# Gated recurrence of a hybrid decoder step: score masks on 32-token diagonal blocks, log k kept, three level buffers, levels by GpSimd

## What is computed

```python
L = jnp.cumsum(lc, axis=2)
inter = jnp.einsum('bhtk,bhkv->bhtv', qc * jnp.exp(L), S)
diff = jnp.where(causal, L[:, :, :, None, :] - L[:, :, None, :, :], -jnp.inf)
A = jnp.einsum('bhtk,bhsk,bhtsk->bhts', qc, kc, jnp.exp(diff))
intra = jnp.einsum('bhts,bhsv->bhtv', A, vc)
L_end = L[:, :, -1:, :]
S = jnp.exp(L_end[:, :, 0, :, None]) * S + jnp.einsum('bhsk,bhsv->bhkv', kc * jnp.exp(L_end - L), vc)
```

## Time and profile before

| | |
|---|---|
| Median of three runs | 2465.13 us (2464.92 to 2468.68) |
| The profiled execution: its time | 2473.21 us |
| Its span, first to last instruction | 2471.3 us |
| Mean granted TensorE clock | 0.961 |
| PE matmul busy | 2330.7 us (94%) |
| DVE busy | 1298.9 us (53%) |
| POOL busy | 1087.2 us (44%) |
| ACT busy | 487.6 us (20%) |
| Chain that ended last | PE 84%, DVE 7%, issue 4%, SP's queue 4%, ACT 1% |

### The profile page before, as it was taken

How to read it: one execution, slowest core, us unless ns; L and a number is a source line. 1 busy time by engine, 2 the same in 40 slices (tenths; PEclk the granted TensorE clock), 3 DMA queues, 4 the chain that set the end, 5 groups by cost and what they waited for, 6 DMA issues and landing times.

```text
span 2471.3 us, 33961 instructions
## 1 busy us (share of the span) xinstructions
PE 2330.7 (94%) x10472; PEld 1793.0 (73%) x10472; DVE 1298.9 (53%) x1975; ACT 487.6 (20%) x916; POOL 1087.2 (44%) x1274
## 2 busy tenths in 40 slices
PE   8998987999998999999899989879999989999997
PEld 6775776677776777777676757667777767777775
DVE  0634687533456666671216347874333666666622
ACT  1534211211113101100125332112111121010002
POOL 0000724556663666734300008254666637676342
PEclk9999986999999999999999999869999999999998
DMA  6222110222212222222032211103221222121220
GB/s 214 80 73 61 39 73 1 104 77 77 77 52 98 85 71 82 80 70 83 35 122 84 81 44 39 73 1 113 77 77 69 69 98 85 68 85 68 77 71 38
DMA packets 51600, 183.60 MB, mean 74 GB/s; under 512 B 7234, under 2 KB 27970, under 8 KB 37762
## 3 DMA queue, kind: packets, MB, share of 16 engines
q1 hardware_dynamic: 50882, 178.49, 21.2%
q10 hardware_dynamic: 576, 3.36, 0.3%
HBM read 172.64 MB, written 9.18 MB: 74 GB/s over the span
## 4 chain that ended last, share of the span: by engine, by line
PE 84%; DVE 7%; issue 4%; SPq 4%; ACT 1%; DMA 0%; POOL 0%; DVEq 0%; ACTq 0%; POOLq 0%
PE ps L1154 23%; PE ps L1082 18%; PE ps L1192 16%; PE ps L857 14%; PE ps L1398 3%; PE ps L1325 1%; PE ps L878 1%; SPq L694 1%; SPq L706 1%; PE ps L1075 1%; DVE r L2171 1%; PE ps L1067 1%; SPq L699 1%; DVE xT L1945 1%; DVE r L634 1%
## 5 line engine op out<-in xcount | busy, mean ns | idle before, releaser
L857 PE MATMUL ps<-xT,wring 128*128 128x288 f32 (+2 forms) x1152 | 282.2, 408 | 1.4 <-DVE o_mla L2112 1.4
L857 PEld LDWEIGHTS ps<-xT,wring 128*128 128x128 f32 x1152 | 219.9, 191 | 62.5 <-issue 1.7
L634 POOL TENSOR_TENSOR r<-lq 128x288 f32<-128x288 f32 (+1 forms) x40 | 28.6, 715 | 530.1 <-PE ps L1426 530.1
L1154 PE MATMUL ps<-lq,mreg 128*128 128x288 f32 x1008 | 251.3, 406 | 0.0
L1154 PEld LDWEIGHTS ps<-lq,mreg 128*128 128x128 f32 x1008 | 191.5, 190 | 52.9
L1507 ACT ACTIVATE r<-ps 128x288 f32<-128x288 f32 (+7 forms) x268 | 113.3, 428 | 562.8 <-PE ps L1082 255.4
L1154 PE MATMUL ps<-xT,wring 128*128 128x288 f32 x672 | 169.8, 406 | 0.0
L1154 PEld LDWEIGHTS ps<-xT,wring 128*128 128x128 f32 x672 | 127.7, 190 | 35.3
L1082 PE MATMUL ps<-r,kbuf 128*128 128x288 f32 x576 | 143.6, 406 | 0.0
L2585 POOL TENSOR_TENSOR kbuf<-o_mla 128x288 f32<-128x288 f32 x42 | 33.3, 792 | 225.6 <-DVE o_mla L2350 225.6
L1082 PEld LDWEIGHTS ps<-r,kbuf 128*128 128x128 f32 x576 | 109.4, 190 | 30.2
(11 more groups left out here) (377 smaller groups left out, 4747.9 us busy)
## 6 DMA issues: line engine op xcount, KB each, us to landing
wring<-w_stream SPq DMA_DIRECT2D x100, 1024.0 KB, 4.9
side<-w_stream SPq DMA_DIRECT2D x18, 704.0 KB, 4.3
r<-pages_in SPq DMA_DIRECT2D x80, 128.0 KB, 2.1
vbuf<-w_stream SPq DMA_DIRECT2D x12, 512.0 KB, 3.7
r<-w_stream SPq DMA_DIRECT2D x12, 512.0 KB, 3.6
wring<-w_stream SPq DMA_DIRECT2D x8, 704.0 KB, 4.2
r<-w_stream SPq DMA_DIRECT2D x6, 704.0 KB, 4.2
mreg<-pages_in SPq DMA_DIRECT2D x32, 128.0 KB, 2.1
```

The source lines that it names most:

```text
L634: eng.tensor_tensor(hi, lhi, mid, ALU.subtract)
L857: mm = pe.matmul(out[0:w.shape[-1], a * 512:a * 512 + hi - lo], w, x[:, lo:hi], start=(k == 0), stop=(k == len(pairs) - 1))
L1154: mm = pe.matmul(up_sum[name], ws[:, k * P:(k + 1) * P], xs[:, k, :], start=(k == 0), stop=(k == HK - 1))
```

## The change

It does seven things.

1. The lower six score blocks (the diagonal and levels 1 to 16) are computed only inside the four 32-token blocks on the diagonal: 24 matmuls of 32x32 for a chunk, each with a 32-column weight tile, in place of the 128x128 ones. The levels 32 and 64 are computed only where they have a pair, in four more matmuls, in a bank of their own. A chunk has 28 matmuls where it had nine.
2. DVE masks 192 columns (L2196 in the changed kernel), sums them into 32 PSUM columns (L2199), and spreads the sum over its own blocks with a 0/1 multiply (L2205).
3. ACT copies the off-diagonal blocks into the scores, three small copies, and PE waits for `hg_full`.
4. log k is kept in place of k (minus the cumulated log f), so that the lower half of a level needs no multiply after its exponential; the k of the diagonal is exponentiated into `k_now`, the decay to the chunk's end by four activations with a bias.
5. There are three level buffers, so head 2's levels are formed during head 0.
6. POOL forms all levels of all heads; DVE has none, and the `late` order is gone. ACT's exponentials for heads 2 and 3 go behind the copies of steps 0, 1, 2, 7 and 10 to 13.
7. The masks in the constants shrink from 1024 to 320 columns, and `value_blocks` is one 64x1024 operation.

The core of the diff:

```diff
+SUB = 32
+N_DIAG = LEVELS.index(SUB) + 1
+LEV_BUF = (2, 0, 1, 2)
+LEVEL_STEPS = {0: (2, 0, 2), 1: (2, 2, 5), 2: (2, 5, 7), 10: (3, 0, 2), 11: (3, 2, 5), 12: (3, 5, 7)}
+END_STEPS = {7: 2, 13: 3}
...
                 lo, hi, _ = parts(out, half)
-                llo, lhi, mid = parts(logf[:, h, 0:n], half)
...
                 eng.tensor_tensor(hi, lhi, mid, ALU.subtract)
-                ins = eng.tensor_tensor(lo, mid, llo, ALU.subtract)
+                ins = eng.tensor_tensor(lo, alo, mid, ALU.add)
...
-                pe.matmul(out[0:w, 0:w], k_hg[:, h, t0:t1], q_hg[:, h, t0:t1], start=True, stop=True)
...
+                for v in range(N_DIAG if c < N_CHUNK else 1 + SMALL_LEVELS):
+                    for i in range(w // SUB):
+                        lo, hi = SUB * i, SUB * (i + 1)
...
+                        mm = pe.matmul(diag[lo:hi, v * SUB:(v + 1) * SUB], k, q, start=True, stop=True)
                 if c < N_CHUNK:
+                    m = lev[N_DIAG]
+                    for i in range(2):
+                        pe.matmul(off[SUB * i:SUB * (i + 1), 0:64], m[:, at + SUB * i:at + SUB * (i + 1)],
+                                  m[:, at + 64:at + P], start=True, stop=True)
...
+                    if c < N_CHUNK:
+                        act.wait_ge(*hg_scores.at(l, n + 1))
+                        full, off = scores_hg[:, n % 2, :], bank[2 * (n % 2) + 1]
+                        copy(full[0:64, 64:P], off[0:64, 0:64])
+                        for a in (0, 64):
+                            ins = copy(full[a:a + SUB, a + SUB:a + 64], off[a:a + SUB, 64:64 + SUB])
+                        ins.then_inc(hg_full.sem, 1)
+                    if n in LEVEL_STEPS:
+                        decays_levels(*LEVEL_STEPS[n])
+                    if n in END_STEPS:
+                        decays_ends(END_STEPS[n])
...
+                    summed = bank[2 * (n % 2)][0:w, N_DIAG * SUB:(N_DIAG + 1) * SUB]
+                    dve.tensor_reduce(summed, masked[0:w, 0:nl, :].rearrange("p l t -> p t l"), AX_X, ALU.add
+                                      ).then_inc(hg_summed.sem, 1)
...
                 for n in range(N_HG + 1):
-                    h, c = divmod(n, N_CHUNK + 1)
-                    late = n < N_HG and c == 0 and h >= 2
...
+                    if n < N_HG:
+                        pair_sums(n)
+                    if n >= 1:
                         update(n - 1)
...
+                pool.wait_ge(*pool_d_ready.at(l, POOL_GROUPS))
+                differences(l, 2)
+                scaled(l, 2)
+
+                pool.wait_ge(*hg_upd.at(l, N_CHUNK + 2))
+                ends(l, 2)
+                value_blocks(l, 1)
+                ends_scaled(l, 2)
+                differences(l, 3)
+
+                pool.wait_ge(*hg_upd.at(l, 2 * (N_CHUNK + 2)))
+                ends(l, 3)
+                value_blocks(l, 2)
+                scaled(l, 3)
+                ends_scaled(l, 3)
```

More of the change, by code:

```diff
@@ L617, in parts, with levels @@
             return v[:, :, 0:half], v[:, :, half:2 * half], v[:, :, half - 1:half]
-        def levels(h, first=0, end=len(LEVELS)):
+        def levels(h, first, end):
+            b = LEV_BUF[h]
             for v in range(first, end):
-                half = LEVELS[v]
+                yield LEVELS[v], level[b][v], 0, SEQ
                 if v < SMALL_LEVELS:
-                    yield half, level_small[h % 2][:, v, :], T
-                else:
-                    yield half, level_big[h % 2][:, v - SMALL_LEVELS, :], SEQ
@@ L628, in level_differences @@
-        def level_differences(eng, h, first, end):
-            for half, out, n in levels(h, first, end):
+                    yield LEVELS[v], level_s[b][v], SEQ, T
+        def level_differences(eng, h, first=0, end=len(LEVELS)):
+            for half, out, t0, t1 in levels(h, first, end):
                 lo, hi, _ = parts(out, half)
-                llo, lhi, mid = parts(logf[:, h, 0:n], half)
-                mid = mid.broadcast_to([P, n // (2 * half), half])
+                _, lhi, mid = parts(logf[:, h, t0:t1], half)
+                alo, _, _ = parts(log_k[:, h, t0:t1], half)
+                mid = mid.broadcast_to([P, (t1 - t0) // (2 * half), half])
@@ L648, in ends_scaled, with level_scaled @@
-        def ends_scaled(eng, h):
-            eng.tensor_tensor(decayed[:, h % 2, 0, :], decayed[:, h % 2, 0, :], q_hg[:, h, :], ALU.mult)
-            return eng.tensor_tensor(decayed[:, h % 2, 1, :], decayed[:, h % 2, 1, :], k_hg[:, h, :], ALU.mult)
+        def level_scaled(eng, h, first=0, end=len(LEVELS)):
+            for half, out, t0, t1 in levels(h, first, end):
+                _, hi, _ = parts(out, half)
+                _, qhi, _ = parts(q_hg[:, h, t0:t1], half)
+                ins = eng.tensor_tensor(hi, hi, qhi, ALU.mult)
+            return ins
@@ L1022, in hg_pair_scores @@
-                if c < N_CHUNK:
-                    for v in range(SMALL_LEVELS, top - 1):
-                        m = big[:, v - SMALL_LEVELS, t0:t1]
-                        pe.matmul(out[:, (v + 1) * P:(v + 2) * P], m, m, start=True, stop=True)
-                    o = top * P
-                    m = big[:, top - SMALL_LEVELS, t0:t1]
-                    pe.matmul(out[:, o:o + P], m, m, start=True, stop=True)
-                    half = LEVELS[top]
+                diag, off = bank[2 * (n % 2)], bank[2 * (n % 2) + 1]
@@ L2481, in value_blocks @@
[L2481 to L2488 removed]
+                level_differences(pool, h).then_inc(lev_diff.sem, 1)
@@ L2836, in shape_constants @@
     s, t = np.arange(P)[:, None], np.arange(P)[None, :]
-    c[:, C_MASK:C_MASK + P] = s == t
-    for v, half in enumerate(LEVELS):
-        same = s // (2 * half) == t // (2 * half)
-        at = C_MASK + min(v + 1, len(LEVELS) - 1) * P
-        c[:, at:at + P] += same & (s % (2 * half) < half) & (t % (2 * half) >= half)
+    inside = SUB * (s // SUB) + np.arange(SUB)[None, :]
+    c[:, C_MASK:C_MASK + SUB] = s == inside
+    for v in range(N_DIAG - 1):
+        half = LEVELS[v]
+        at = C_MASK + (v + 1) * SUB
+        c[:, at:at + SUB] = ((s // (2 * half) == inside // (2 * half)) & (s % (2 * half) < half)
+                             & (inside % (2 * half) >= half))
+    c[:, C_BLOCKS:C_BLOCKS + P] = s // SUB == t // SUB
     tok = np.arange(T)
```

241 lines of the change are left out of this document (116 added, 125 removed).

## The result

The changed kernel takes **2391.64 us** (median of four runs, 2390.33 to 2393.01). Four runs of the kernel before have a median of 2466.49, which makes 74.9 us less. The later runs bear it out: there the kernel before had medians of 2470.1 to 2472.4, and the changed kernel, run again, a ratio of 0.9679. I had said 43 less. The direction was right and the size was not: the recurrence saves 41 us a layer, where I had worked out 21.5.

What follows compares the result with a forecast made beforehand. PE's queue and its waits bound the kernel, with DVE the fuller engine in the recurrence: PE's queue 27.5 us shorter a layer, less 6 of POOL waits, nets 21.5, 43 in all; 2465.1 becomes 2422 us, range 2391 to 2460.

Steps and rivals of the forecast that it cites:

- DVE stops being the bound: Recurrence, each chunk: DVE's mask, sum and spread take 1.1 us in place of 2.8; a chunk every 1.5 us.
- I take 31 ns: PE's 56 small-matmul instructions a chunk start 31 ns apart at full clock: 1.7 us, 2.0 with the transpose.
- Hidden, by 0.7 us: ACT's score copies: scores complete 2.1 us after the last pair score, while PE has 2.8 us of other work.
- if the small matmuls were free this would be the bound: Remark on the recurrence: the path through DVE and ACT's copies, 2.1 us, would bound if small matmuls cost nothing.
- The wait ahead of head 3: Recurrence: PE waits 5.0 us for POOL's multiplies, which follow ACT's last exponentials, before head 3's first step.
- The wait of 0.7 ahead of head 2: Recurrence: POOL is done 34.9 us into the stage, PE wants head 2 at 34.2, so PE waits 0.7 us.
- At nothing: Outside the recurrence: forming log k, loading constants and POOL's runs ahead of the stage were charged no time.
- A: Rival: small matmuls at 57 ns, twice that at half clock, become the bound; +7.5 us a layer, 2480 us; chance 0.12.
- B: Rival: PE at half clock for the whole recurrence; 3.5 us less a layer, 2458 us; chance 0.12.
- C: Rival: POOL and ACT set the recurrence's pace; waits 15 us a layer, not 6; 2440 us; chance 0.16.
- D: Rival: the clock stays at 2.4 GHz in the recurrence; 14 us more saved a layer, 2393 us; chance 0.15.
- the 56 instructions last 1.7 us: Sign of being right: a chunk's 56 small-matmul instructions on PE take 1.7 us at full clock.

Runs made afterwards that it cites:

- Run 1: Changed kernel with the 24 diagonal matmuls of a chunk issued block by block, not walking through the four blocks in turn; ratio 0.9729 to the kernel before.

## Why the prediction was right and wrong

- **DVE stops being the bound: right.** Its three operations, 9.6 us in a head and the vanished waits are as worked out. The 1.09 us put back at each chunk, of the 1.7 that had gone, are worth 7 us a layer, since PE or ACT comes next.
- **PE, "I take 31 ns": this is the step that failed.** It measured 12 ns at full and 20 at half clock, where I had 31 and 55. The rows I read it from had 64-column weights and two places; four places and 32 columns are outside what they show, and I noted "half the columns" without letting it lower the number. I also misread what told the two rows apart: the four instructions at 57 ns (L956) write to the two halves in turn just as L1426 does, so in those rows the places don't explain 57 against 31. Ten chunks a layer by 1.0 us and six by 2.1 make 22.6 us less PE work. I set an upper end (57 ns, with a rival of its own) and no lower one. Run 1 shows what the order of the four blocks carries: without it the distance is 23 ns, so 11 of the 19 ns between 31 and 12. The other 8 no run explains.
- **The copies, "Hidden, by 0.7 us": wrong, as a consequence.** The 1.7 us of pair scores that were to hide them took 0.69. The remark behind it, "if the small matmuls were free this would be the bound", was right, and it decided how much of those 22.6 us came out. The copies cost waits of 6.1 us in layer 0, part of them behind ACT's exponentials (2.16 ahead of the pair scores of step 9, behind the 2.8 us of head 2's ends) and behind the table load of 1.28, for which I had charged nothing.
- **The wait ahead of head 3: right** at 5.5 and 5.2 us for 5.0, with all earlier starts shifted, since it hangs on ACT's steps, which follow PE's. The wait of 0.7 ahead of head 2 didn't come.
- **The account** in layer 0: 96.0 us predicted - 22.6 + 6.1 = 79.5; the sample scores took 0.51 in place of 0.9 (1.6 in four) and head 0's 512-column products ran at full clock (1.8): 76.1. But eight chunks ran at half clock and one changed over, not six, which puts about 1 us back: 77 beside 76.8 measured.
- **At nothing: right.** Outside the recurrence the change is 0.2 us.
- **The rivals.** A (small matmuls dear) and B (half clock throughout) are out. (By the prediction's own sums A decides from 64 ns, not 61.) C was true in part as a mechanism, waits for ACT and POOL of 11.6 us a layer, beside a gain that I had missed. D named almost the measured time, 2393, for a wrong reason: the mean clock in the stage is 0.74, and was 0.75. The range's lower end, 2391, came from D and owes its nearness to luck. The median of 2391.64 is just above it, but the ratio of 0.9677, held against the 2465.13 that I had started from, is 2385.5 and below it, and down there I had nothing. Of the signs of being wrong that I had listed none would have caught this; of those of being right, "92 to 100 us in each layer" and "the 56 instructions last 1.7 us" did.

## What to carry to other kernels

A long row of small matmuls is priced by the distance of starts, and that depends on whether neighbours write to different 32-row blocks: here 12 ns in turn and 23 ns block by block. When the nearest rows differ in kind from the new instruction, give the price a lower end too. When two engines pass a chunk back and forth, a cut on one is worth only part of itself: of the work put back on DVE here, 0.40 came out in the time, whether PE had its load or not. After that, the order of the helpers' queues (ACT's steps, POOL's) is the next thing to move, and it gave 22 us here for a few lines. Look for table loads in the trace of ACT: the first exponential behind another function had one of 1.28 us, in the middle of a loop that waits for ACT's copies.

## What I had not expected of the hardware

- Instructions with 32-column weights to four blocks in turn start 12 ns apart at full clock, 20 at half; 104 of them took 1.18 us.
- PE can stand without a semaphore to wait for: 3.2 us in the middle of small matmuls, with the DMA engines 98% busy, when a chunk had 104 such instructions. The changed kernel, with 56, had no such gap, and with the same 56 block by block there was one of 0.86 us in layer 0 and one of 0.40 in layer 1. The cause is not shown.
- Eight products over 64 columns take 2.00 us where 8 columns took 1.95, and after them the clock fell less often: the stage's granted clock was 0.93 (window 320 to 395 of layer 0) for 0.76, and in layer 1 (1497 to 1570) 0.84.
